# Low parts of the gate projections' weights: by a subtraction on VectorE, or by transfers that add the raw weights to the negated high part

## The chip, the cores and the metric

The kernel runs on one core of a Trainium2 chip. Such a core has TensorE (PE) for matrix products, VectorE (DVE), ScalarE (ACT) and GpSimd (POOL) for elementwise work, SyncE (SP), which here only issues transfers, and 16 DMA engines. Each engine works through its own list of instructions in order; they wait for each other on semaphores. SyncE and GpSimd each have a queue of transfers of their own. The metric is the device time of one execution in microseconds (us), the median of several runs.

## The reference, cut to what matters

Two layers of a hybrid decoder trunk on 528 prompt tokens and 64 sample tokens (592 columns in all), in float32. One input projection of the normalized x yields queries, keys, values, the gates of two branches and two merging gates g_a and g_b:

```python
def mixer_layer(x, ...):
    xn = rmsnorm(x, ln_g)
    proj = xn @ w_in
    q, k, v, z_a, x_b, z_b, g_a, g_b = jnp.split(proj, SPLIT_IDX, axis=-1)
    ...
    o_a = group_norm(ret, gn_g).astype(x.dtype) * jax.nn.silu(z_a)
    xc, conv_new = causal_conv(x_b, conv_buf, cw, cb)
    h, h_last = rglru(xc, h0, w_r, b_r, w_i, b_i, lam)
    o_b = h.astype(x.dtype) * jax.nn.silu(z_b)
    merged = jax.nn.sigmoid(g_a) * (o_a @ w_a) + jax.nn.sigmoid(g_b) * (o_b @ w_b)
    return x + merged @ w_o, S_new, conv_new, h_last
```

The change concerns the weights of g_a and g_b: 2 x 1024 columns of w_in, 1024 deep, per layer.

## The kernel before

**Numbers in two parts.** Products of float32 are made from pairs: every operand is split in a high part, rounded to the type that TensorE multiplies (fp32r), and a low part, the rest. A product is then three matmuls: high by high, low by high, high by low (`three`, lines 1654 to 1659).

**The stream of weights.** All weights of a layer come as 124 units of 128 x 1024 numbers (512 KB) in the order in which they are used. There is a ring of four slots (RING = 4). SyncE loads unit u into slot u % 4 of `w_raw` as soon as TensorE has ended unit u - 4 (lines 541 to 552). ScalarE copies it to `w_hi` (`split_hi`, line 464), VectorE subtracts `w_hi` from `w_raw` (`split_lo`, line 472) and counts up the semaphore unit_lo, for which TensorE waits ahead of the unit (`wait_unit`). `w_lo` and `w_raw` are the same memory: the subtraction is done in place. Both splits of unit i + 3 stand, in each engine's list, behind the engine's own work on unit i.

**The phases of a layer** are R (four heads of retention, 16 units each), L (the convolution and the gated recurrence, 24 units in two passes), GA and GB (the projections g_a and g_b, 8 units each, numbered 88 to 103 within the layer), B (the product with w_b, 12 units) and O (w_o, 8 units). In GA and GB each unit makes two halves of 296 columns (288 in the last layer). ScalarE takes each half out of PSUM with a tanh into `sg` (`tanh_g`, line 934), which frees its bank; there are four banks, two units' worth, so unit 90 needs those of unit 88. VectorE multiplies `sg` of GA into `acc` (line 1552). In GB the same goes on, but first ScalarE makes the twelve high parts of `ob` (line 990) and VectorE the twelve low ones (line 1557).

**The end of phase L** reaches into GA. The last group's recurrence is three scans on VectorE (`scan`, lines 1493 to 1508); they need ScalarE's exponentials and roots (lines 974 to 984), which follow ScalarE's splits of units 90 and 91. The third scan stands behind VectorE's split of unit 92.

**GpSimd's list** at that place, which is also the order of its transfers: the transfers that mix tiles for the gates of the recurrence (`mixes`, line 662), a wait for the last scan (ob_ready), then four transfers: the old x to `xT` (2368 KB), the next layer's parameters, the convolution outputs and the recurrence outputs to DRAM; then a wait until the latter two have been stored (lru_out), then, in layer 0, a wait for the new x (lines 686 to 699).

```python
act.wait_ge(unit_in[n % RING], arrived(l * UNITS_LAYER + it * p.units + p.unit0 + n))
act.activation(w_hi[:, n % RING, :], w_raw[:, n % RING, :], ACT.Copy).then_inc(unit_hi, 1)
...
dve.wait_ge(unit_hi, l * UNITS_LAYER + it * p.units + (p.unit0 + n + 1))
dve.tensor_tensor(w_lo[:, n % RING, :], w_raw[:, n % RING, :], w_hi[:, n % RING, :].bitcast(f32),
                  SUB).then_inc(unit_lo, 1)
```

Of the kernel before, what the change touches and what calls it, by code (L numbers as in the profile page):

```python
# [46 lines left out]
RING = 4  # L47
# [174 lines left out]
def trunk(nc, x_in, w_units, gate_w, packs, final_gain, consts, decay, state_ret,  # L222
          y_out, ret_p, ret_s, conv_out, h_out):
    f32, f32r = mybir.dt.float32, mybir.dt.float32r
    ALU, ACT = mybir.AluOpType, mybir.ActivationFunctionType
    MUL, ADD, SUB = ALU.mult, ALU.add, ALU.subtract
# [3 lines left out]
    with ctx:  # L230
# [3 lines left out]
        def keep(name, shape, dt=f32):  # L234
            at = (top[0] + 31) // 32 * 32
            top[0] = at + int(np.prod(shape[1:])) * 4
            return nc.alloc_sbuf_tensor_at(name, shape, dt, offset=at)
# [5 lines left out]
        w_hi = keep("w_hi", [P, RING, 1024], f32r)  # L243
        top[0] = (top[0] + 31) // 32 * 32
        w_raw = alias("w_raw", top[0], [P, RING, 1024])
        w_lo = keep("w_lo", [P, RING, 1024], f32r)
# [113 lines left out]
        def sem(name):  # L360
            return ctx.enter_context(nc.semaphore(name))

        unit_in = [sem(f"unit_in{i}") for i in range(RING)]
        unit_hi, unit_lo, unit_done = sem("unit_hi"), sem("unit_lo"), sem("unit_done")
# [1 line left out]
        bank_free = [sem(f"bank_free{i}") for i in range(RING)]  # L366
        const_in, trig_in, ones_ready, x_ready, x_stored, x_again = (sem(n) for n in (
            "const_in", "trig_in", "ones_ready", "x_ready", "x_stored", "x_again"))
        gain_in = sem("gain_in")
        xgh_ready, xg_ready = sem("xgh_ready"), sem("xg_ready")  # L370
        x_init = [sem(f"x_init{i}") for i in range(len(LOADS))]
        first_in, first_hi_ready, first_lo_ready, eps_ready = (sem(n) for n in (
# [45 lines left out]
        def apart(eng):  # L418

            eng.sem_inc(passed, 1)  # L420
# [33 lines left out]
        def v_bank(j):  # L454
            return psum_of("R", ("v", j)) if j < 4 else v_last

        def split_hi(act, ph, l, it, i):

            p = PH[ph]
            n = i + AHEAD  # L460
            if l * UNITS_LAYER + it * p.units + p.unit0 + n >= UNITS:
                return
            act.wait_ge(unit_in[n % RING], arrived(l * UNITS_LAYER + it * p.units + p.unit0 + n))
            act.activation(w_hi[:, n % RING, :], w_raw[:, n % RING, :], ACT.Copy).then_inc(unit_hi, 1)  # L464

        def split_lo(dve, ph, l, it, i):
            p = PH[ph]
            n = i + AHEAD
            if l * UNITS_LAYER + it * p.units + p.unit0 + n >= UNITS:
                return  # L470
            dve.wait_ge(unit_hi, l * UNITS_LAYER + it * p.units + (p.unit0 + n + 1))
            dve.tensor_tensor(w_lo[:, n % RING, :], w_raw[:, n % RING, :], w_hi[:, n % RING, :].bitcast(f32),  # L472
                              SUB).then_inc(unit_lo, 1)
# [96 lines left out]
        def _(pool):  # L570
# [13 lines left out]
            for l in range(0, DEPTH):  # L584
# [80 lines left out]
                def mixes(g):  # L665
                    gg = l * GROUPS + g
                    pool.wait_ge(gw_free, l * 6 + g + 2)
                    for tiles_done, parts in ((2, ((0, 0, 96, 128), (0, 1, 0, 96), (1, 1, 64, 128))), (3, ((1, 2, 0, 64),))):
                        for which, ready in enumerate((xch_ready, xcl_ready)):
                            pool.wait_ge(ready, gg * 3 + tiles_done)  # L670
                            apart(pool)
                            for to, tile, r0, r1 in parts:
                                mix(g, to, tile, r0, r1, which)
# [9 lines left out]
                load_gates(3)  # L683
                mixes(2)
                mixes(3)
                pool.wait_ge(ob_ready, l * LT + LT)
                apart(pool)
                pool.dma_start(xT[:, :, :].rearrange("p k t -> p (k t)"), x_in if l == 0 else x_scr[l - 1])\
# [5 lines left out]
                               h_new[:, :, :].rearrange("p a b -> p (a b)")).then_inc(lru_out, 16)  # L694
                pool.wait_ge(lru_out, l * 32 + 32)
                pool.sem_inc(lru_left, 1)
                if l + 1 < DEPTH:
                    pool.wait_ge(x_ready, l * KT + KT)
                    pool.dma_start(x_scr[l], acc[:, :, :].rearrange("p k t -> p (k t)")).then_inc(x_stored, 16)
# [1414 lines left out]
```

## Time and profile before

| | |
|---|---|
| median of 3 runs | 1926.42 us (1926.24 to 1926.42) |
| the profiled execution | 1926.77 us |
| its span, from the first to the last instruction | 1924.9 us |
| TensorE busy | 1904.5 us, 99% of the span |
| VectorE busy | 1187.7 us, 62% |
| ScalarE busy | 760.9 us, 40% |
| GpSimd busy | 267.5 us, 14% |
| GpSimd's transfers | 95.22 MB, 14.9% of the engines' time |
| SyncE's transfers | 149.71 MB, 24.9% |

The times of busy engines overlap, so they don't add up to the span. The engine that is busy throughout sets it; of the others one has to ask whether it ever makes that one wait. A timeline row reads: start, duration, engine, line of the program, operation, result and operands with their shapes, and in brackets how long the engine stood idle before it and what ended that. A line of waits reads: engine, what it was about to do, for whom it waited; the total, how many times, and the longest. Transfers issued by GpSimd have a row of their own for the issue; the time from there to the landing of the last byte is listed with the transfers.

### The profile page before, as it was taken

What the parts mean: (1) busy time and instruction counts of PE and PEld (TensorE: products, weight loads), DVE (VectorE), ACT (ScalarE), POOL (GpSimd) and SP (SyncE); (2) the same over time, 40 slices, a digit from 0 to 9 for tenths busy, and PEclk for the clock granted to TensorE, in tenths of its full rate; (3) what the DMA queues carried; (4) which work ended last, traced back from release to release, by engine and by line L of the source; (5) the groups of instructions that cost most, each with busy time, mean ns of one, the idle gap of its engine ahead of it and who ended that gap; (6) DMA issues with size and microseconds to landing.
All of it is one profiled execution on the core that took longest, in us unless ns stands there. A gap on an engine that the chain in (4) does not pass through costs nothing.

```text
span 1924.9 us, 32032 instructions
## 1 busy us (share of the span) xinstructions
PE 1904.5 (99%) x13112; PEld 1782.1 (93%) x13112; DVE 1187.7 (62%) x2008; ACT 760.9 (40%) x1181; POOL 267.5 (14%) x375
## 2 busy tenths in 40 slices
PE   8999999999999999999999999999999999999998
PEld 7889898898899999999998988988988999999997
DVE  8775665665766887424487656657557678763345
ACT  5432322323327776422344223233123377754223
POOL 2221120120231200000022201202102422000000
PEclk9999999999999999999999999999999999999999
DMA  6435534453443433322254435534444533342222
GB/s 216 133 117 164 169 136 127 161 174 111 146 149 93 114 99 113 113 77 77 88 172 156 139 127 171 171 114 146 164 127 135 163 102 110 92 138 77 87 79 82
DMA packets 105857, 246.99 MB, mean 128 GB/s; under 512 B 10830, under 2 KB 51262, under 8 KB 105326
## 3 DMA queue, kind: packets, MB, share of 16 engines
q1 hardware_dynamic: 78590, 149.71, 24.9%
q0 software_dynamic: 26976, 95.22, 14.9%
q8 instruction: 104, 1.70, 0.4%
q14 instruction: 43, 0.35, 0.1%
q10 hardware_dynamic: 144, 0.00, 0.0%
HBM read 186.07 MB, written 49.12 MB: 122 GB/s over the span
## 4 chain that ended last, share of the span: by engine, by line
PE 85%; DVE 5%; ACT 4%; DVEq 2%; DMA 1%; ACTq 1%; issue 1%; SPq 0%
PE bank L1657 21%; PE bank L1659 20%; PE bank L1658 20%; PE bank L1727 4%; PE bank L1729 4%; PE bank L1728 4%; PE last L1745 1%; PE last L1727 1%; PE last L1729 1%; PE last L1728 1%; PE sums L1852 1%; PE sums L1854 1%; PE sums L1856 1%; PE bank L1908 1%; PE sums L1763 1%
## 5 line engine op out<-in xcount | busy, mean ns | idle before, releaser
L1657 PE MATMUL bank<-xn_hi,w_hi 128*128 128x296 f32 (+1 forms) x2432 | 726.7, 299 | 0.2
L1659 PE MATMUL bank<-xn_lo,w_hi 128*128 128x296 f32 (+1 forms) x2432 | 722.3, 297 | 0.0
L1658 PE MATMUL bank<-xn_hi,w_lo 128*128 128x296 f32 (+1 forms) x2432 | 721.5, 297 | 0.0
L1657 PEld LDWEIGHTS bank<-xn_hi,w_hi 128*128 128x128 f32 x2432 | 457.3, 188 | 6.6 <-issue 4.3
L1658 PEld LDWEIGHTS bank<-xn_hi,w_lo 128*128 128x128 f32 x2432 | 457.7, 188 | 1.1
L1659 PEld LDWEIGHTS bank<-xn_lo,w_hi 128*128 128x128 f32 x2432 | 456.8, 188 | 0.0
L472 DVE TENSOR_TENSOR w_lo<-w_raw,w_hi 128x1024 fp32r<-128x1024 f32 x245 | 300.3, 1228 | 186.2 <-ACT w_hi L464 179.3
L464 ACT ACTIVATE w_hi<-w_raw 128x1024 fp32r<-128x1024 f32 x245 | 257.8, 1055 | 353.8 <-DMA w_raw<-in_w_units 349.3
L1657 PE MATMUL bank<-oa_hi,w_hi 128*128 128x296 f32 (+1 forms) x512 | 153.7, 300 | 0.0
L1658 PE MATMUL bank<-oa_hi,w_lo 128*128 128x296 f32 (+1 forms) x512 | 151.9, 297 | 0.0
L1659 PE MATMUL bank<-oa_lo,w_hi 128*128 128x296 f32 (+1 forms) x512 | 151.7, 296 | 0.0
L1657 PE MATMUL bank<-ob_hi,w_hi 128*128 128x296 f32 (+1 forms) x384 | 113.9, 297 | 0.0
L1658 PE MATMUL bank<-ob_hi,w_lo 128*128 128x296 f32 (+1 forms) x384 | 113.9, 297 | 0.0
L1659 PE MATMUL bank<-ob_lo,w_hi 128*128 128x296 f32 (+1 forms) x384 | 113.8, 296 | 0.0
L1727 PE MATMUL bank<-w_hi,xn_hi 128*128 128x512 f32 x256 | 100.8, 394 | 0.7 <-DVE rot_k L1191 0.7
L1729 PE MATMUL bank<-w_lo,xn_hi 128*128 128x512 f32 x256 | 100.8, 394 | 0.0
L1728 PE MATMUL bank<-w_hi,xn_lo 128*128 128x512 f32 x256 | 100.7, 393 | 0.0
L1657 PEld LDWEIGHTS bank<-oa_hi,w_hi 128*128 128x128 f32 x512 | 96.3, 188 | 3.9 <-issue 3.9
L1658 PEld LDWEIGHTS bank<-oa_hi,w_lo 128*128 128x128 f32 x512 | 96.3, 188 | 0.0
L1659 PEld LDWEIGHTS bank<-oa_lo,w_hi 128*128 128x128 f32 x512 | 96.3, 188 | 0.0
L606 POOL DMA_DIRECT2D out_ret_s<-S x64 | 46.0, 721 | 326.5 <-DVEq L1142 181.4
L781 ACT ACTIVATE zz<-bank 128x296 f32<-128x296 f32 (+1 forms) x64 | 26.6, 415 | 133.3 <-PE bank L1659 132.7
(293 smaller groups left out, 3069.0 us busy)
## 6 DMA issues: line engine op xcount, KB each, us to landing
w_raw<-in_w_units SPq DMA_DIRECT2D x215, 512.0 KB, 3.6
S<-in_state_ret POOLq DMA_DIRECT2D x64, 512.0 KB, 4.7
out_ret_s<-S POOLq DMA_DIRECT2D x64, 512.0 KB, 6.3
w_raw<-in_w_units SPq DMA_DIRECT2D x66, 256.0 KB, 3.3
vst<-v_scr SPq DMA_DIRECT2D x8, 512.0 KB, 4.0
out_ret_p<-Sp POOLq DMA_DIRECT2D x8, 512.0 KB, 5.7
v_scr<-vtok_hi SPq DMA_DIRECT2D x16, 160.0 KB
dec<-in_decay POOLq DMA_DIRECT2D x9, 264.0 KB, 5.0
```

What stands on the lines that cost most here:

```text
L464: act.activation(w_hi[:, n % RING, :], w_raw[:, n % RING, :], ACT.Copy).then_inc(unit_hi, 1)
L472: dve.tensor_tensor(w_lo[:, n % RING, :], w_raw[:, n % RING, :], w_hi[:, n % RING, :].bitcast(f32), SUB).then_inc(unit_lo, 1)
L606: pool.dma_start(dst, S[:, s, :, :]).then_inc(s_out[s], 16)
L781: act.activation(zz[:, i - 8, a:b], psum_of("R", name)[:, 0:b - a], ACT.Tanh, scale=0.5)\
L1657: pe.matmul(ps, w_hi[:, slot, cols], x_hi, start=first, stop=False)
L1658: pe.matmul(ps, w_lo[:, slot, cols], x_hi, start=False, stop=False)
L1659: return pe.matmul(ps, w_hi[:, slot, cols], x_lo, start=False, stop=last)
L1727: pe.matmul(ps, left_hi, right_hi, start=first, stop=False)
L1728: pe.matmul(ps, left_lo, right_hi, start=False, stop=False)
L1729: return pe.matmul(ps, left_hi, right_lo, start=False, stop=last)
L1745: ins = pe.matmul(o_last[at:at + QUAD, :], qz[:, c, b * QUAD:b * QUAD + QUAD], S[:, s, c, :], start=(n < 4 and c == 0), stop=(n >= 4 and c ...
L1763: return pe.matmul(to[:, :], kst[rows, b // 4, c * P:c * P + P], vst[rows, b // 4, :], start=True, stop=True)
```

## The change

In units 88 to 103 of each layer the low part is made in another way. ScalarE, behind the high part, drains and writes the negated high part over the raw weights (`w_lo`, the same memory). GpSimd then issues a transfer that reads the raw weights of the unit from DRAM a second time and adds them to what is there, so that raw minus high is left. VectorE no longer subtracts in these units; at the same place in its list it waits for the transfer and passes it on to TensorE by counting up unit_lo. The adds of the first five units stand in GpSimd's list ahead of its wait for the last scan, the other eleven behind the wait for the stores.

```diff
--- before.py
+++ after.py
@@ -366,7 +366,7 @@
         bank_free = [sem(f"bank_free{i}") for i in range(RING)]
         const_in, trig_in, ones_ready, x_ready, x_stored, x_again = (sem(n) for n in (
             "const_in", "trig_in", "ones_ready", "x_ready", "x_stored", "x_again"))
-        gain_in = sem("gain_in")
+        gain_in, minus_hi, lo_in = sem("gain_in"), sem("minus_hi"), [sem(f"lo_in{i}") for i in range(RING)]
         xgh_ready, xg_ready = sem("xgh_ready"), sem("xg_ready")
         x_init = [sem(f"x_init{i}") for i in range(len(LOADS))]
         first_in, first_hi_ready, first_lo_ready, eps_ready = (sem(n) for n in (
@@ -454,6 +454,11 @@
         def v_bank(j):
             return psum_of("R", ("v", j)) if j < 4 else v_last
 
+        GATED = range(PH["GA"].unit0, PH["GB"].after[1])
+
+        def gated(l, at):
+            return l * len(GATED) + at - GATED.start
+
         def split_hi(act, ph, l, it, i):
 
             p = PH[ph]
@@ -462,11 +467,19 @@
                 return
             act.wait_ge(unit_in[n % RING], arrived(l * UNITS_LAYER + it * p.units + p.unit0 + n))
             act.activation(w_hi[:, n % RING, :], w_raw[:, n % RING, :], ACT.Copy).then_inc(unit_hi, 1)
+            if it * p.units + p.unit0 + n in GATED:
+                act.drain()
+                act.activation(w_lo[:, n % RING, :], w_hi[:, n % RING, :].bitcast(f32), ACT.Copy, scale=-1.0)\
+                   .then_inc(minus_hi, 1)
 
         def split_lo(dve, ph, l, it, i):
             p = PH[ph]
             n = i + AHEAD
             if l * UNITS_LAYER + it * p.units + p.unit0 + n >= UNITS:
+                return
+            if it * p.units + p.unit0 + n in GATED:
+                dve.wait_ge(lo_in[n % RING], 16 * (gated(l, it * p.units + p.unit0 + n) // RING + 1))
+                dve.sem_inc(unit_lo, 1)
                 return
             dve.wait_ge(unit_hi, l * UNITS_LAYER + it * p.units + (p.unit0 + n + 1))
             dve.tensor_tensor(w_lo[:, n % RING, :], w_raw[:, n % RING, :], w_hi[:, n % RING, :].bitcast(f32),
@@ -683,6 +696,15 @@
                 load_gates(3)
                 mixes(2)
                 mixes(3)
+
+                def add_raw(at):
+                    pool.wait_ge(minus_hi, gated(l, at) + 1)
+                    apart(pool)
+                    pool.dma_start(w_lo[:, at % RING, :], w_units[l * UNITS_LAYER + at], accum_op=ADD)\
+                        .then_inc(lo_in[at % RING], 16)
+
+                for at in GATED[0:5]:
+                    add_raw(at)
                 pool.wait_ge(ob_ready, l * LT + LT)
                 apart(pool)
                 pool.dma_start(xT[:, :, :].rearrange("p k t -> p (k t)"), x_in if l == 0 else x_scr[l - 1])\
@@ -694,6 +716,8 @@
                                h_new[:, :, :].rearrange("p a b -> p (a b)")).then_inc(lru_out, 16)
                 pool.wait_ge(lru_out, l * 32 + 32)
                 pool.sem_inc(lru_left, 1)
+                for at in GATED[5:]:
+                    add_raw(at)
                 if l + 1 < DEPTH:
                     pool.wait_ge(x_ready, l * KT + KT)
                     pool.dma_start(x_scr[l], acc[:, :, :].rearrange("p k t -> p (k t)")).then_inc(x_stored, 16)
```

In GpSimd's list, from the last mixing transfers of layer 0 to the end of the layer, stood before:

```order
L662 DMA mix_hi<-xc_hi 64x592 [waits xch_ready]
L662 DMA mix_lo<-xc_lo 64x592 [waits xcl_ready]
L688 DMA xT<-in_x 128x4736 [waits ob_ready]
L690 DMA lp<-in_packs 128x504
L691 DMA out_conv<-conv_new 128x324
L693 DMA out_h<-h_new 128x108
L699 DMA x_scr<-acc 128x4736 [waits lru_out,x_ready]
```

and stands now:

```order
L675 DMA mix_hi<-xc_hi 64x592 [waits xch_ready]
L675 DMA mix_lo<-xc_lo 64x592 [waits xcl_ready]
L703 DMA w_lo<-in_w_units 128x1024 [waits minus_hi] x5
L710 DMA xT<-in_x 128x4736 [waits ob_ready]
L712 DMA lp<-in_packs 128x504
L713 DMA out_conv<-conv_new 128x324
L715 DMA out_h<-h_new 128x108
L703 DMA w_lo<-in_w_units 128x1024 [waits lru_out,minus_hi]
L703 DMA w_lo<-in_w_units 128x1024 [waits minus_hi] x10
L723 DMA x_scr<-acc 128x4736 [waits x_ready]
```

The wait for the stores (lru_out) has moved from the transfer of the new x to the add of unit 93.

In VectorE's list, from the end of the second scan of the last group (layer 0) through the third to the first products with `sg`, stood before:

```order
L1508 SCALAR_TENSOR_TENSOR ob<-rr,zl 128x592
L472 TENSOR_TENSOR w_lo<-w_raw,w_hi 128x1024 [waits unit_hi]
L1493 TENSOR_TENSOR ii<-ii,rr 128x592 [waits sqrt_ready]
...
L1508 SCALAR_TENSOR_TENSOR ob<-rr,ob 128x592
L1552 SCALAR_TENSOR_TENSOR acc<-sg,acc 128x296 [waits ga_ready] x4
L472 TENSOR_TENSOR w_lo<-w_raw,w_hi 128x1024 [waits unit_hi]
```

and stands now:

```order
L1532 SCALAR_TENSOR_TENSOR ob<-rr,zl 128x592
L1517 TENSOR_TENSOR ii<-ii,rr 128x592 [waits lo_in0,sqrt_ready]
...
L1532 SCALAR_TENSOR_TENSOR ob<-rr,ob 128x592
L1576 SCALAR_TENSOR_TENSOR acc<-sg,acc 128x296 [waits ga_ready] x4
L1576 SCALAR_TENSOR_TENSOR acc<-sg,acc 128x296 [waits lo_in1,ga_ready]
```

The subtraction for unit 92 has gone from between the scans, and its place is taken by a wait for the add of unit 92 (lo_in0) ahead of the third scan; that for unit 93 (lo_in1) stands among the products.

In ScalarE's list, where the high parts of units 90 and 91 are made in layer 0, stood before:

```order
L917 ACTIVATE ii<-bank,lp 128x592 [waits psum_full]
L464 ACTIVATE w_hi<-w_raw 128x1024 [waits unit_in2]
L464 ACTIVATE w_hi<-w_raw 128x1024 [waits unit_in3]
L917 ACTIVATE rr<-sums,lp 64x592 [waits psum_full]
```

and stands now:

```order
L941 ACTIVATE ii<-bank,lp 128x592 [waits psum_full]
L469 ACTIVATE w_hi<-w_raw 128x1024 [waits unit_in2]
L472 ACTIVATE w_lo<-w_hi 128x1024
L469 ACTIVATE w_hi<-w_raw 128x1024 [waits unit_in3]
L472 ACTIVATE w_lo<-w_hi 128x1024
L941 ACTIVATE rr<-sums,lp 64x592 [waits psum_full]
```

Each high part is followed by its negation, ahead of the gates of the recurrence.

## Rows read from the trace of the kernel before

**Rows 1.** The page, busy time (share of the span) and instructions of each engine.

```profile
PE 1904.5 (99%) x13112; PEld 1782.1 (93%) x13112; DVE 1187.7 (62%) x2008; ACT 760.9 (40%) x1181; POOL 267.5 (14%) x375
```

**Rows 2.** The waits of TensorE: us in total, times, longest us.

```profile
PE bank L1657 <- DVE xg_lo L1063: 1.8, 2, 1.1
...
PE last L1727 <- DVE w_lo L472: 0.7, 1, 0.7
```

**Rows 3.** The page, costliest groups: busy us, mean ns | idle before, releaser.

```profile
L472 DVE TENSOR_TENSOR w_lo<-w_raw,w_hi 128x1024 fp32r<-128x1024 f32 x245 | 300.3, 1228 | 186.2 <-ACT w_hi L464 179.3
```

**Rows 4.** Timeline of TensorE: first matmuls of units 88, 90, 92, 93, 99; layer 1: 93, 99.

```profile
735.94 0.30 PE L1657 MATMUL bank<-xn_hi,w_hi 128*128 128x296 f32 x1
...
748.98 0.30 PE L1657 MATMUL bank<-xn_hi,w_hi 128*128 128x296 f32 x1
...
762.02 0.30 PE L1657 MATMUL bank<-xn_hi,w_hi 128*128 128x296 f32 x1
...
768.54 0.30 PE L1657 MATMUL bank<-xn_hi,w_hi 128*128 128x296 f32 x1
...
807.66 0.30 PE L1657 MATMUL bank<-xn_hi,w_hi 128*128 128x296 f32 x1
...
1715.89 0.29 PE L1657 MATMUL bank<-xn_hi,w_hi 128*128 128x288 f32 x1
...
1754.13 0.29 PE L1657 MATMUL bank<-xn_hi,w_hi 128*128 128x288 f32 x1
```

**Rows 5.** Timeline of ScalarE around GA and GB, layer 0, then layer 1.

```profile
736.71 2.01 ACT L464 ACTIVATE w_hi<-w_raw 128x1024 fp32r<-128x1024 f32 x2
...
748.00 0.40 ACT L934 ACTIVATE sg<-bank 128x296 f32<-128x296 f32 x1
...
754.78 1.06 ACT L464 ACTIVATE w_hi<-w_raw 128x1024 fp32r<-128x1024 f32 x1
...
798.09 1.06 ACT L464 ACTIVATE w_hi<-w_raw 128x1024 fp32r<-128x1024 f32 x1
...
1702.92 1.06 ACT L464 ACTIVATE w_hi<-w_raw 128x1024 fp32r<-128x1024 f32 x1
...
1744.82 1.06 ACT L464 ACTIVATE w_hi<-w_raw 128x1024 fp32r<-128x1024 f32 x1
```

**Rows 6.** The page, DMA issues: KB of each, median us from issue to landing.

```profile
S<-in_state_ret POOLq DMA_DIRECT2D x64, 512.0 KB, 4.7
```

**Rows 7.** Stretch with xT: each engine's busy us, PEclk, DMA share, GB/s.

```profile
763.00:770.00 7.00, 7.00 (x53) 7.00 (x53) 5.50 (x11) 2.38 (x4) 2.22 (x4) 1.00 0.93 321
```

**Rows 8.** Timeline of GpSimd, layer 0, then layer 1.

```profile
729.16 0.52 POOL L662 DMA_DIRECT2D mix_lo<-xc_lo  x1 [0.28 <-issue]
763.83 0.58 POOL L688 DMA_DIRECT2D xT<-in_x  x1 [34.15 <-DVE ob L1508]
...
765.50 0.55 POOL L693 DMA_DIRECT2D out_h<-h_new  x1
...
1711.90 0.58 POOL L688 DMA_DIRECT2D xT<-x_scr  x1 [34.14 <-DVE ob L1508]
...
1713.57 0.55 POOL L693 DMA_DIRECT2D out_h<-h_new  x1
```

**Rows 9.** Timeline of VectorE: first instruction of the third scan, layer 0.

```profile
759.64 0.78 DVE L1493 TENSOR_TENSOR ii<-ii,rr 128x592 f32<-128x592 f32 x1
```

**Rows 10.** DMA issues in 760 to 790 us, then in 1708 to 1735 us.

```profile
out_h<-h_new POOLq DMA_DIRECT2D x1, 54.0 KB, 11.4
...
out_h<-h_new POOLq DMA_DIRECT2D x1, 54.0 KB, 9.8
```

**Rows 11.** Last stretches: busy us (PE first), then PEclk, DMA share, GB/s.

```profile
1916.00:1917.00 1.00, 0.39 (x2) 0.00 (x0) 0.04 (x1) 0.51 (x2) 0.00 (x0) 1.00 0.12 40
...
1919.00:1920.00 1.00, 0.00 (x0) 0.00 (x0) 1.00 (x2) 0.00 (x0) 0.00 (x0) 1.00 0.00 0
1920.00:1921.00 1.00, 0.00 (x0) 0.00 (x0) 1.00 (x2) 0.00 (x0) 0.00 (x0) 0.86 0.31 115
1921.00:1921.50 0.50, 0.00 (x0) 0.00 (x0) 0.50 (x2) 0.00 (x0) 0.00 (x0) 0.50 1.06 362
```

## The prediction

> **What bounds the kernel now.** I read the table of busy times first, then the waits of TensorE, then the timeline of each engine around the gate units of layer 0 (735 to 808 us) and of layer 1 (1684 to 1754 us). TensorE is busy for 99% of the span [rows 1]. Its waits are tiny: the longest sum in the list is 1.8 us, and the one wait for a low part in a stage after the first units is 0.7 us in total [rows 2]. So nothing that VectorE gives up can shorten the run by more than a microsecond or so; the question is only whether the new way of making the low parts is ever late. A unit that comes late stops TensorE, and nearly all of that delay goes to the end, since TensorE has no idle time elsewhere in which to make it up.
>
> I call the sixteen gate units of a layer 88 to 103, as the code numbers them. **What is removed:** 32 subtractions on VectorE, 1.23 us each [rows 3], 39 us of VectorE's time. VectorE is busy for 62% [rows 1], and TensorE hardly waits for it, so I price this at zero.
>
> **The deadlines.** From TensorE's timeline: unit 88 starts at 735.94, 90 at 748.98, 92 at 762.02, 93 at 768.54 and 99 at 807.66; in layer 1, 93 starts at 1715.89 and 99 at 1754.13 [rows 4]. A unit lasts 6.52 us in layer 0 and 6.37 in layer 1 (the second follows from 1715.89 and 1754.13, six units apart).
>
> **What is added on ScalarE:** behind each high part a wait for its own result and a second pass of the same size, 1.06 us [rows 5], with its drain 1.1 us. In the middle of the sixteen this is nothing, because ScalarE idles there. At the head it is not: the high parts of 90 and 91 are made back to back from 736.71, and everything behind them follows without a gap up to the high part of 92 at 754.78 [rows 5]. So from there ScalarE runs 2.2 us later. The first sigmoid-gate evacuation (line 934) moves from 748.00 to 750.2 and frees its bank at 750.6, where TensorE wants it at 748.98 for unit 90 [rows 4, 5]: a first delay of 1.6 us. The high part of 92 begins at 757.0 instead of 754.78, its negation ends at 759.2.
>
> **What is added on the transfer queue:** 32 accumulating transfers of 512 KB, issued by GpSimd. The trace has no such transfer. The nearest rows: plain loads of 512 KB that GpSimd issues take 4.7 us from issue to landing [rows 6]. That is the lower bound, since the new ones move the same bytes. An accumulating transfer has to read its destination too. Between 763 and 770 us the engines moved 321 GB/s at a share of 0.93, so 345 GB/s when fully busy [rows 7]; one more reading of 512 KB is then 1.5 us, which gives 6.2 us. The upper bound is a transfer of twice the whole plain time, 9.4 us. I take **L = 6.2 us**: start-up and completion are paid once, only the movement doubles.
>
> The Trainium skill bears on this in two places. "DMA: Bandwidth & Descriptors" (Anatomy of one DMA — SWDGE (gpsimd) path) fits a GpSimd-issued transfer as about 2.0 us plus bytes over 436 GB/s, which would be 3.2 us here; this trace says 4.7, and the trace decides. "Collectives: The Full Stack" (The bandwidth ceiling: the fold count and why AG ≠ RS ≠ AR) says that an add in the transfer engines halves the rate because it needs two source reads, not because adding costs time; by it and the fit together L would be an estimated 4.4 us (3.2 and another 1.2 for the second reading), and the sum below, with its four L, some 7 us smaller. No row of this trace shows an add, so the rule is untested here.
>
> **What is moved: the place of the transfers in GpSimd's order.** This is the term that decides. GpSimd handles its list strictly in order. The adds of 88 to 92 stand ahead of its wait for the last scan; the add of 93 stands behind it, and behind the wait until the convolution and recurrence outputs have been stored (lru_out). Before, no one cared how late that was.
>
> Unit 88: GpSimd is busy with the last mixing transfer until 729.7 [rows 8]; 729.7 + 6.2 = 735.9, against 735.94. A few tenths at most, which the 1.6 us of ScalarE's shift cover. Units 89 to 91 have 6.5 us more each. VectorE now stands waiting for the adds of 88 to 91 until about 748, but the work behind it waits for ScalarE until about then anyway.
>
> Unit 92: negated at 759.2, add issued 759.3, landed 765.5, VectorE goes on at 765.6. TensorE, already 1.6 us late, wanted it at 763.6, so it is now 3.7 us late. More important is what is queued behind VectorE's wait: the third scan. It began at 759.64 [rows 9] and GpSimd issued the first of its four transfers at 763.83 [rows 8], 4.2 us later. Now: 765.6 + 4.2 = 769.8.
>
> Unit 93: the four transfers (xT, lp, conv, h) are issued one after the other, the last at 765.50, 1.67 us after the first [rows 8], and that last one landed 11.4 us after its issue [rows 10], together 13.1 us, since it stands behind 2.4 MB of xT. 769.8 + 13.1 = 782.9: the add of 93 is issued. + 6.2 = 789.1, + 0.2 for VectorE's passing it on = 789.3. It was wanted at 768.54: **TensorE is 20.8 us late**, the 3.7 us and 1.6 us included. It stands idle from about 772 to 789. In terms of L this is 8.4 + 2 L, as two adds lie one behind the other on the path.
>
> Layer 1 in the same way: high part of 92 at 1702.92 + 2.2 = 1705.1 [rows 5], negated 1707.3, landed 1713.6, VectorE 1713.7, GpSimd 1717.9. There the four transfers took from 1711.90 to 1713.57 + 9.8 [rows 8, 10], 11.5 us: 1729.4. Add landed 1735.6, TensorE 1735.8 against 1715.89 [rows 4]: **19.9 us late**, or 7.5 + 2 L.
>
> Units 94 and 95 were negated long before and their adds follow that of 93 directly; even at 3 us between landings they are in time. From 96 on the chain is: TensorE ends unit i, ScalarE evacuates, makes high part and negation of i+3 (done 2.8 us after the end), the add takes 6.2: 9.2 us with the passing on, of the 13.0 us (two units) that there are. Hidden, with 3.8 us to spare; what uses that up is L above 10 us.
>
> Unit 99 is the exception, because ScalarE first makes the twelve high parts of ob. Its own high part began at 798.09 [rows 5], now 799.2; negated 801.4, landed 807.7, passed on 807.9, wanted 807.66: 0.2 us. In layer 1, 1744.82 [rows 5] leads to 1754.6 against 1754.13 [rows 4]: 0.5 us. Together 0.7.
>
> **The clock.** After the last matmuls of the kernel (two of them in 1916 to 1917) the granted clock stays at 1.00 until 1920 and then falls to 0.50, as the mean of 0.86 in 1920 to 1921 tells [rows 11]: 2.4 GHz, then 1.2 GHz, some 4 us after the last work. In a hole of 17 us the same must happen, and TensorE starts unit 93 at half speed. How fast it comes back no row shows. Bounds: nothing, and one whole unit at half speed, 6.5 us. If the clock rises about as quickly as it fell, it costs half of 4 us: I take 2 us a layer, 4 in all.
>
> **The sum.** 20.8 + 19.9 + 0.7 + 4.0 = 45.4 us. The profiled execution took 1926.77 us (span 1924.9), which is within 0.4 of the median 1926.42. 1926.8 + 45.4 = **1972 us**.
>
> **Rivals.**
> (a) The adds are much slower than any row suggests, L = 14 us. Then the head costs 36.4 + 35.5, and the steady part no longer hides: each three units lose 14 + 3 - 13 = 4 us, unit 99 about 8, some 16 us a layer. 1926.8 + 72 + 32 + 4 = 2035 us. For: nothing in the trace adds in a transfer. Against: the bytes. It decides from L = 10 on.
> (b) The add of 93 isn't held up: GpSimd's wait for the stores is over in time and only ScalarE's 1.6 us a layer stays. 1930 us. Against: even on the times of before, the stores landed at 765.50 + 11.4 = 776.9, 8.4 us after unit 93 began, so this needs a wrong reading of GpSimd's order.
> (c) The other side, a little faster: all adds hidden, and VectorE's freed 39 us take away TensorE's small waits. The place is the head of each layer's recurrence, where VectorE is crowded; but the gated subtractions come after most of it. At most 1 us: 1926 us, no change. It decides only if (b) holds as well and ScalarE's shift is absorbed.
> (d) The change doesn't do what it says, for example VectorE still subtracts or the adds aren't there. The instruction lists show 16 adds a layer and no subtraction in their place, so this has no chance worth a number.
>
> **How the numbers follow.** Forecast 0.85, (a) 0.11, (b) 0.02, (c) 0.02, of which half would read as faster at all. The forecast's own range: L = 4.7 and no cost of the clock give 17.8 + 16.9 = 34.7, so 1961; L = 9.4 gives 27.2 + 26.3, unit 99 a further 7, and the clock up to 13: 73.5, so 2000. I widen it a little to both sides, for stores that land sooner or later than before and for a part of (a): 1958 to 2006. A measurement of this kernel can tell about 0.2% from no change, 3.9 us. Faster 0.01, the same 0.02, slower 0.97.
>
> **What will show it.** Right: in the waits, TensorE stands once per layer for some 17 us ahead of its first instruction on unit 93, near 772 to 789, and again near 1742 to 1758 in layer 1, whose clock times are some 23 us later by then; in the waits of VectorE two long ones, for the adds of 92 and 93; GpSimd's first add behind out_h about 13 us after xT was issued; the adds' time from issue to landing near 6 us; the granted clock at 0.50 in the hole and for a few us after it; unit 96 to 98 with no wait. Wrong: TensorE's hole missing; adds landing in under 4.7 us or over 10 us; many waits of some 4 us spread over the gate units (then (a)); a hole that costs no clock.

## The result, and the profile after

| | before | after |
|---|---|---|
| median | 1926.42 us (1926.24 to 1927.38, 4 runs) | 1972.88 us (1970.94 to 1977.13, 4 runs) |
| the profiled execution | 1926.77 us | 1972.85 us |
| TensorE busy | 1904.5 us, 99% | 1911.3 us, 97% |
| VectorE busy | 1187.7 us | 1151.5 us |
| ScalarE busy | 760.9 us | 793.9 us |

The kernel became slower: the ratio after to before is 1.0243, 95% interval 1.0225 to 1.0261. The forecast was 1972 us, 1958 to 2006. The 36 us that VectorE gave up bought nothing, and TensorE stood some 40 us longer. The costliest groups of the page after (busy us, mean ns | idle before, releaser) and its transfers (KB, median us from issue to landing):

```profile
L1681 PE MATMUL bank<-xn_hi,w_hi 128*128 128x296 f32 (+1 forms) x2432 | 729.8, 300 | 39.4 <-DVEq L482 38.6
...
L485 DVE TENSOR_TENSOR w_lo<-w_raw,w_hi 128x1024 fp32r<-128x1024 f32 x213 | 261.2, 1229 | 156.5 <-ACT w_hi L469 100.6
...
w_lo<-in_w_units POOLq DMA_DIRECT2D x32, 512.0 KB, 5.7
```

The subtraction on VectorE [rows 3] is down from 245 to 213 times. L482 is the line in which VectorE counts up unit_lo after an add has landed, and it ends 38.6 of the 39.4 us in which TensorE stood before a unit's first matmul. The waits of TensorE and VectorE after (total us, times, longest), against [rows 2]:

```profile
DVE acc L1576 <- DMA w_lo<-in_w_units: 87.8, 12, 17.4
...
PE bank L1681 <- DVEq L482: 38.6, 8, 15.8
```

Where the eight are, the timeline of TensorE says (start, duration, ..., idle before and releaser). These are the first matmuls of units 88, 90, 92, 93 and 99 of layer 0, then 88, 90, 92, 93 and 99 of layer 1, against [rows 4]:

```profile
737.18 0.41 PE L1681 MATMUL bank<-xn_hi,w_hi 128*128 128x296 f32 x1 [1.19 <-DVEq L482]
...
750.69 0.37 PE L1681 MATMUL bank<-xn_hi,w_hi 128*128 128x296 f32 x1 [0.20 <-ACT sg L958]
...
765.21 0.41 PE L1681 MATMUL bank<-xn_hi,w_hi 128*128 128x296 f32 x1 [1.24 <-DVEq L482]
...
787.03 0.61 PE L1681 MATMUL bank<-xn_hi,w_hi 128*128 128x296 f32 x1 [15.04 <-DVEq L482]
...
829.58 0.41 PE L1681 MATMUL bank<-xn_hi,w_hi 128*128 128x296 f32 x1 [0.49 <-DVEq L482]
...
1707.44 0.40 PE L1681 MATMUL bank<-xn_hi,w_hi 128*128 128x288 f32 x1 [1.53 <-DVEq L482]
...
1720.99 0.38 PE L1681 MATMUL bank<-xn_hi,w_hi 128*128 128x288 f32 x1 [0.54 <-ACT sg L958]
...
1735.46 0.40 PE L1681 MATMUL bank<-xn_hi,w_hi 128*128 128x288 f32 x1 [1.48 <-DVEq L482]
...
1757.90 0.61 PE L1681 MATMUL bank<-xn_hi,w_hi 128*128 128x288 f32 x1 [15.80 <-DVEq L482]
...
1800.15 0.40 PE L1681 MATMUL bank<-xn_hi,w_hi 128*128 128x288 f32 x1 [1.79 <-DVEq L482]
```

Two rows carry 31 of the 39 us: one hole per layer, both before unit 93. What leads to the hole in layer 0 stands in the chain of work that released unit 93 (start, duration, what; "DMA" runs from the end of the waiting to the landing):

```profile
758.09 1.07 ACT w_lo L472
759.20 0.53 issue
759.72 5.39 DMA w_lo<-in_w_units
...
765.30 0.78 DVE ii L1517
...
766.49 1.39 DVE rr L1526
...
768.19 0.69 DVE ob L1532
768.92 0.55 issue
769.47 0.56 POOL xT L710
...
771.10 9.51 DMA out_h<-h_new
...
780.75 0.54 issue
781.31 5.63 DMA w_lo<-in_w_units
786.96 0.03 DVEq L482
...
787.03 0.61 PE bank L1681
```

Read from the top: ScalarE ends the negation of unit 92; its add lands 5.4 us after the issue; only then does VectorE begin the third scan (765.30, against 759.64 in [rows 9]); GpSimd issues its four transfers; the last one lands 9.5 us after its issue; only then is the add of unit 93 issued; 5.6 us later TensorE may go on. Of the computation in these rows only the first is new. The rest of the chain is two adds, and between them a wait that nobody had to care about before.

### The profile page after: what moved, and what is told of

It is laid out like the page before. It is cut to its first block, busy times and chain, and to the rows that moved or that the text cites. A ratio compares the mean times of both kernels' runs of the same rounds, so it can differ in the third digit from the quotient of the medians.

```text
span 1971.0 us, 32160 instructions
## 1 busy us (share of the span) xinstructions
PE 1911.3 (97%) x13112; PEld 1786.7 (91%) x13112; DVE 1151.5 (58%) x1976; ACT 793.9 (40%) x1213; POOL 295.4 (15%) x407
## 4 chain that ended last, share of the span: by engine, by line
PE 78%; ACT 6%; DVE 6%; DMA 4%; ACTq 2%; issue 2%; DVEq 2%; SPq 0%; POOL 0%; POOLq 0%
PE bank L1681 19%; PE bank L1683 18%; PE bank L1682 18%; PE bank L1751 4%; PE bank L1753 4%; PE bank L1752 4%; DMA w_lo<-in_w_units 2%; PE last L1769 1%; PE last L1751 1%; PE last L1753 1%; PE last L1752 1%; DMA out_h<-h_new 1%; ACT w_hi L469 1%; PE sums L1876 1%; PE sums L1878 1%
## 5 line engine op out<-in xcount | busy, mean ns | idle before, releaser
L1681 PE MATMUL bank<-xn_hi,w_hi 128*128 128x296 f32 (+1 forms) x2432 | 729.8, 300 | 39.4 <-DVEq L482 38.6
L485 DVE TENSOR_TENSOR w_lo<-w_raw,w_hi 128x1024 fp32r<-128x1024 f32 x213 | 261.2, 1229 | 156.5 <-ACT w_hi L469 100.6
```

Source lines behind the costliest of these rows:

```text
L1681: pe.matmul(ps, w_hi[:, slot, cols], x_hi, start=first, stop=False)
```

## The experiments

The runs came in three groups. Those of a group were on one chip and share runs of the kernel before on it: 1926.22 us for the four on all adds first, the wait behind, the scan first and the passes alone; 1926.05 us for xT behind, the transfers without addition, TensorE kept busy (its first run) and the part without six units; 1926.19 us for the last three (the two repeats and the six units alone). Ratios are to that. Which line numbers a kernel has depends on its edit: "DVEq L482" is VectorE's passing on, "sg" ScalarE's evacuation of a bank.

The theory (T): the place of the adds in GpSimd's list makes the holes, by way of the chain above; ScalarE's second pass, the time of one add and the clock are small terms. The rivals: (R1) it is the adding itself, which is slow in the DMA engines; (R2) it is ScalarE's second passes; (R3) it is the clock that the holes cost.

### All adds ahead of the wait for the last scan

```diff
-                for at in GATED[0:5]:
+                for at in GATED:
                     add_raw(at)
...
                 pool.sem_inc(lru_left, 1)
-                for at in GATED[5:]:
-                    add_raw(at)
```

> All sixteen adds of a layer stand ahead of GpSimd's wait for the last scan and of the four transfers. My theory: both holes of 15 us go and the clock stays at full speed; what is left are the short waits of the kernel as changed, ahead of 88 (1.2 and 1.5 us), 90 (0.2 and 0.5), 92 (1.2 and 1.5) and 99 (0.5 and 1.8), 8.4 us in all: 1935 us. Rival, that the adds are too slow for two units' time (13 us): waits of several us at each of 94 to 98 as well, over 1950 us.

Measured: 1939.35 us (1937.32 to 1943.0), ratio 1.007 (1.0056 to 1.0084). The same 32 adds and the same passes of ScalarE, in another place, cost 13.1 us instead of 46.5. The waits of TensorE in this kernel:

```profile
PE bank L1679 <- DVEq L482: 6.4, 6, 1.4
PE bank L1679 <- DVE w_lo L485: 2.2, 2, 1.1
...
PE bank L1679 <- ACT sg L956: 1.1, 2, 0.8
```

There is no hole any more. What is left is 6.4 us for late adds (88, 92 and 99), 1.1 us for banks, and a new one, 2.2 us for a subtraction: the raw weights of unit 105 come late, since xT's 2.4 MB now move beside them. The row of ScalarE's timeline in layer 0:

```profile
842.66 1.06 ACT L469 ACTIVATE w_hi<-w_raw 128x1024 fp32r<-128x1024 f32 x1 [4.68 <-DMA w_raw<-in_w_units]
```

Unit 105 counts here since TensorE waits for units 104 and 105 together at the head of phase B. This rules out R1 and R2 as the main cause: both are whole in this kernel. The median came out some 4 us above what T expected. The three waits sum to 9.7 us; the profiled execution, at 1937.32 us the fastest of the four, was 11.1 us slower than before. What the slower ones spent beyond that no trace shows.

### The wait for the stores moved behind the adds

```diff
-                pool.wait_ge(lru_out, l * 32 + 32)
-                pool.sem_inc(lru_left, 1)
                 for at in GATED[5:]:
                     add_raw(at)
+                pool.wait_ge(lru_out, l * 32 + 32)
+                pool.sem_inc(lru_left, 1)
```

> The wait for the stores (lru_out) is moved behind the adds of units 93 to 103; the four transfers (xT, lp, conv, h) stay ahead of them. My theory: about half of the hole ahead of unit 93 goes, because the add no longer waits for a completion, but it stays behind 2.4 MB of xT in the same queue. xT was issued at 769.5 and took 9.0 us; the add then lands near 781 to 782 instead of 787, so 5 to 6 us less per layer: 1961 to 1963 us. Rival, that transfers of one queue don't hold each other up: the add lands 5.7 us after its issue at 771.7, so near 777.4, 9.6 us less per layer: 1953 us. Rival, that GpSimd's order is not the cause (the adds' own cost is): no change, 1973 us.

Measured: 1965.51 us (1964.55 to 1967.64), ratio 1.0205 (1.0191 to 1.0219). GpSimd's timeline around 771 us, and the issues between 769 and 773 us (KB, us to landing):

```profile
771.28 1.85 POOL L703 DMA_DIRECT2D w_lo<-in_w_units  x2
```

```profile
xT<-in_x POOLq DMA_DIRECT2D x1, 2368.0 KB, 9.4
w_lo<-in_w_units POOLq DMA_DIRECT2D x2, 512.0 KB, 13.1
```

The adds are now issued 10 us sooner (771.28 against 781.31), but the first two land 13.1 us later, not 5.7. They stand behind xT in the same queue, and at 1965.5 us the kernel is a little slower than the 1961 to 1963 that were expected. Unit 93 still waits 11.85 us (12.93 in layer 1). So of the 46.5 us the wait instruction itself accounts for 7; what the instruction waits for, the 2.4 MB ahead, does its harm in either place. To read the hole as "it waits for a semaphore" would have been wrong: moving the wait away doesn't move the bytes away.

### xT behind the adds

```diff
                 apart(pool)
-                pool.dma_start(xT[:, :, :].rearrange("p k t -> p (k t)"), x_in if l == 0 else x_scr[l - 1])\
-                    .then_inc(x_again, 16)
...
                 for at in GATED[5:]:
                     add_raw(at)
+                pool.dma_start(xT[:, :, :].rearrange("p k t -> p (k t)"), x_in if l == 0 else x_scr[l - 1])\
+                    .then_inc(x_again, 16)
```

> Only the transfer of 2.4 MB to xT is moved, behind the adds of 93 to 103; the stores and the wait for them stay ahead of these. My theory: the stores took 9.5 us because they stand behind xT in the queue; alone they land some 4 us after their issue, and one issue of 0.55 us goes as well, so the add of 93 goes out 6 us sooner: 12 us less for both layers, 1961 us, less about 2 us that xT costs where it now stands (at the end of the adds, beside a load of raw weights, as in the kernel with the adds first). Rival, that the stores are slow by themselves: 1973 us.

Measured: 1959.15 us (1957.67 to 1961.84), ratio 1.0174 (1.0158 to 1.0189). GpSimd and TensorE at unit 93:

```profile
770.46 0.57 POOL L713 DMA_DIRECT2D out_h<-h_new  x1
774.50 2.67 POOL L703 DMA_DIRECT2D w_lo<-in_w_units  x3 [3.48 <-DMA out_h<-h_new]
```

```profile
779.94 0.61 PE L1681 MATMUL bank<-xn_hi,w_hi 128*128 128x296 f32 x1 [8.08 <-DVEq L482]
```

Without xT ahead of it the add of 93 is issued 4.0 us after the last store's issue, not 10.2 us (771.10 to 781.31), and the hole shrinks from 15.04 to 8.08 us. The loss is 33.1 us, so 13.4 of the 46.5 are xT's bytes ahead of the stores, less what xT costs where it now stands.

### The third scan ahead of VectorE's wait for unit 92

```diff
-                split_lo(dve, "GA", l, 0, 1)
                 scan(1, 1, 2)
+                split_lo(dve, "GA", l, 0, 1)
```

> Only VectorE's order is changed: the third scan stands ahead of its passing on of unit 92, as it can be done by then. GpSimd's order is that of the changed kernel. My theory: the link from the add of 92 to the third scan carries 4.7 us of each layer (VectorE stood 4.73 and 4.72 us there), so the four transfers and the add of 93 all come that much sooner: 9 us less, 1963 us. Rival, that the scan isn't in the chain: 1973 us.

Measured: 1965.45 us (1963.91 to 1967.85), ratio 1.0202 (1.0187 to 1.0218). GpSimd's timeline:

```profile
764.31 0.55 POOL L710 DMA_DIRECT2D xT<-in_x  x1 [4.25 <-DVE ob L1532]
...
765.94 0.56 POOL L715 DMA_DIRECT2D out_h<-h_new  x1
778.72 2.67 POOL L703 DMA_DIRECT2D w_lo<-in_w_units  x3 [12.21 <-DMA out_h<-h_new]
```

Counted from the issue of the add of 92 (759.21 here, 759.72 in the changed kernel), xT goes out 4.7 us sooner, as expected. The add of 93 doesn't go out 4.7 us sooner: from the issue of out_h to that of the add it is now 12.8 us, before it was 10.2. So the add of 93 moves by only 2.1 us (2.7 in layer 1). By the medians VectorE's wait ahead of the scan is worth some 7 us in all, of which TensorE's waits for adds show 4.9 (33.7 us against 38.6); about half of the sooner start is given back in the queue. What slows the stores there no run separates; the raw weights of SyncE's queue move at that time.

### ScalarE's second passes alone

```diff
+            if it * p.units + p.unit0 + n in GATED:
+                act.activation(w_hi[:, n % RING, :], w_raw[:, n % RING, :], ACT.Copy)
+                act.drain()
             act.activation(w_hi[:, n % RING, :], w_raw[:, n % RING, :], ACT.Copy).then_inc(unit_hi, 1)
```

This is an edit of the kernel before. The high part of these units is made twice, there are no adds, and VectorE subtracts as before.

> ScalarE's extra passes alone: each of the 32 units' high parts is made twice, with a drain between; no adds, VectorE subtracts as before. My theory: 2.2 us later on ScalarE at the head of GA frees the bank of unit 88 late for unit 90 by 1.7 us (layer 0) and 1.9 us (layer 1): 1930 us. Rival, that the ScalarE passes are hidden everywhere: 1926.4 us; rival, that they cost their own 34 us: 1960 us.

Measured: 1931.21 us (1929.88 to 1934.79, 7 runs), ratio 1.0027 (1.0016 to 1.0038). The wait is where it should be, before unit 90 of either layer:

```profile
PE bank L1672 <- ACT sg L949: 3.9, 2, 2.3
```

R2 is worth 4 to 5 us, a tenth. In the changed kernel nearly all of it is covered: unit 88 is late there by itself, so that TensorE wants the bank later.

### The addition taken out of the transfers

```diff
-                    pool.dma_start(w_lo[:, at % RING, :], w_units[l * UNITS_LAYER + at], accum_op=ADD)\
+                    pool.dma_start(w_lo[:, at % RING, :], w_units[l * UNITS_LAYER + at])\
```

The transfers write the raw weights over the negated high part, so what is left out is the addition, and with it the right low parts; order and bytes written are the same.

> The 32 transfers are plain loads of the same 512 KB in place of adds; this leaves out the addition, so the low parts are the raw weights. My theory: the cost of adding is the difference of 5.7 to 4.8 us in landing, and it stands twice in each layer's chain: some 4 us less, 1969 us. Rival, that the addition is what makes the kernel slower: back below 1940 us.

Measured: 1964.63 us (1961.91 to 1966.65), ratio 1.02 (1.0186 to 1.0213). The transfers of this kernel's page, and its waits of TensorE:

```profile
w_lo<-in_w_units POOLq DMA_DIRECT2D x32, 512.0 KB, 3.9
```

```profile
PE bank L1681 <- DVEq L482: 28.4, 3, 14.6
...
PE bank L1681 <- ACT sg L958: 3.6, 2, 1.9
```

Plain transfers land after 3.9 us, adding ones after 5.7: adding costs 1.8 us each. I had expected half of that, as I took the plain one to be 4.8 like the loads of S. Two adds per layer lie on the path to unit 93, so 4 x 1.8 = 7.2 us, and 7.9 were measured (46.5 less this kernel's 38.6). R1 is real and small: with free additions the kernel would still be 38.6 us slower than before. And the 3.6 us of ScalarE's banks come back as soon as unit 88 is in time.

### TensorE kept busy ahead of unit 93

```diff
                         for i in range(4):
+                            if (ph, it, i) == ("GA", 1, 1):
+                                pe.wait_ge(gate_free, 24 * (l + 1))
+                                for _ in range(105):
+                                    pe.matmul(sums[0][:, 0:HALF], xn_hi[:, 0, 0:P], xn_hi[:, 0, 0:HALF],
+                                              start=True, stop=True)
                             project(ph, l, it, ("proj", i), i)
```

The products are used by nobody. They fill the hole, so what is left out is the clock's fall alone.

> As the kernel as changed, but TensorE runs 105 products of 128 x 296 into a free bank ahead of its wait for unit 93, some 14 us of work that nobody uses, where it stood idle for 15.0 and 15.8 us. My theory of the clock: it stays at full speed, and unit 93, which took 5.9 us and 4.2 us at 1.2 GHz in the two layers, gives back half of that: 3.0 + 2.1 = 5 us less, 1968 us. Rival, that the half-speed stretch is hidden by something else that is late (units 94 and 95's adds): no change, 1973 us. Rival, that the extra products run over the wait: longer.

Measured: 1969.93 us (1968.55 to 1973.14), ratio 1.023 (1.0216 to 1.0244). Its distance to the 1972.88 of the changed kernel is no larger than the latter's own spread, so both were run again together:

> The kernel as changed once more, so that the next run is compared with it on the same chip: 1972 us, between 1970 and 1977 as before.

> The same kernel as e5_kept_busy (products that nobody uses in TensorE's hole ahead of unit 93), beside the changed kernel on one chip. Theory of the clock: 5 us less than that one, from half of the 5.9 and 4.2 us that unit 93 takes at 1.2 GHz. Rival, that part of it is hidden: 3 us less or under, as the first comparison over two chips had it.

Measured: the changed kernel 1973.71 us (1973.11 to 1974.11), ratio 1.0247 (1.0233 to 1.0261); with the products 1967.85 us (1967.7 to 1969.86), ratio 1.0219 (1.0205 to 1.0233). The difference is 5.9 us. It is the clock's share and a little more: unit 93 of layer 0 started 0.9 us sooner in the profile of the second. In the first pair part of the gain was lost: in that run's profile with the products, unit 88 of layer 1 came 3.0 us late, and after it the granted clock was 0.61 in 1706 to 1708 and 0.54 in 1708 to 1710. The second profile shows no such stretch. In stretches (us, PE busy first, then the other engines, then PEclk, DMA share, GB/s), the first profile of the changed kernel, then the second one with the products:

```profile
774.00:776.00 2.00, 0.00 (x0) 0.00 (x0) 0.00 (x0) 0.85 (x1) 0.00 (x0) 0.96 0.94 403
776.00:777.00 1.00, 0.00 (x0) 0.00 (x0) 0.00 (x0) 0.00 (x0) 0.00 (x0) 0.50 1.17 495
787.00:788.00 1.00, 0.97 (x4) 0.97 (x5) 0.84 (x2) 0.00 (x0) 0.00 (x0) 0.50 1.11 221
792.00:793.00 1.00, 1.00 (x6) 1.00 (x5) 0.84 (x2) 0.00 (x0) 0.00 (x0) 0.54 0.00 0
793.00:795.00 2.00, 2.00 (x17) 2.00 (x16) 0.00 (x0) 0.42 (x1) 0.00 (x0) 1.00 0.00 0
```

```profile
776.00:777.00 1.00, 1.00 (x10) 1.00 (x9) 0.00 (x0) 0.00 (x0) 0.00 (x0) 1.00 0.95 407
786.00:788.00 2.00, 1.45 (x10) 1.45 (x11) 0.84 (x2) 0.00 (x0) 0.00 (x0) 1.00 0.96 184
```

In the changed kernel TensorE's last matmul ends at 772.0; the mean of 0.96 in 774 to 776 says that the granted clock went from 1.00 to 0.50 (2.4 to 1.2 GHz) at about 775.8. It is 0.50 when unit 93 starts, and back at 1.00 from 792.9 on, after 5.9 us of work at half speed (4.4 us in layer 1). In the timeline the matmuls start 0.25 us apart at 0.50 and 0.14 us apart at 1.00 (0.24 and 0.13 in layer 1), so some 45% of that time is lost, a little less than the half that was expected: 2.6 + 2.0 = 4.6 us. R3 is a tenth of the loss by the trace and an eighth by the two runs.

### Adds only where they are hidden

Here only a part of the sixteen units keeps the new way; the others are subtracted as before. (Not shown: the counts of the semaphores follow the new list, and VectorE drains ahead of the first passing on behind a subtraction.) First units 93 to 98 and 100 to 103, with 93 to 98 ahead of the four transfers and the rest behind the stores:

```diff
-        GATED = range(PH["GA"].unit0, PH["GB"].after[1])
+        GATED = [u for u in range(PH["GA"].unit0 + 5, PH["GB"].after[1]) if u != PH["GB"].unit0 + 3]
...
-                for at in GATED[0:5]:
+                for at in GATED[0:6]:
                     add_raw(at)
```

> The new way only where the timeline shows it hidden: units 93 to 98 and 100 to 103 of each layer, with the six adds of 93 to 98 ahead of the four transfers and the wait for the stores, four behind them. Units 88 to 92 and 99 are subtracted on VectorE as before. My theory: no wait of TensorE is added, and the 20 subtractions that VectorE no longer does (25 us) gain nothing: 1926 to 1927 us, the same as before. Rival, that VectorE's freed time is worth something: under 1924 us. Rival, that a second read of the weights or the transfers' presence costs something everywhere: over 1930 us.

Measured: 1929.09 us (1927.91 to 1929.58, 11 runs), ratio 1.0014 (1.0005 to 1.0023). I had expected no wait at all. TensorE waits 1.8 us for two adds, those of unit 100, whose raw weights came late in either layer. The load of unit 100 in layer 0 and what ScalarE waited for it:

```profile
w_raw<-in_w_units SPq DMA_DIRECT2D x1, 512.0 KB, 9.8
...
803.61 1.06 ACT L472 ACTIVATE w_hi<-w_raw 128x1024 fp32r<-128x1024 f32 x1 [2.79 <-DMA w_raw<-in_w_units]
```

In the kernel before the load of that unit took 3.4 us. Here xT, which the six adds ahead of it have moved to 791.24, goes through the DMA engines at that time; in layer 1 the load took 12.0 us, and ScalarE waited 5.11 us. The 1.2 us that the time is above the two waits no trace places. Then 93 to 98 alone:

```diff
-        GATED = range(PH["GA"].unit0, PH["GB"].after[1])
+        GATED = list(range(PH["GA"].unit0 + 5, PH["GB"].unit0 + 3))
```

> The new way for units 93 to 98 alone (12 of the 32), all ahead of the four transfers. In e8 the waits of TensorE that remained, 0.8 and 1.0 us, stood ahead of unit 100, whose add came behind the transfers. Theory: without it nothing is left, 1926 us, the same as before. Rival, that the transfers' place or the double reading costs by itself what e8 showed beyond its two waits (about 1.2 us): 1927 to 1928 us.

Measured: 1926.32 us (1925.83 to 1927.46, 11 runs), ratio 1.0001 (0.9992 to 1.001). TensorE waits for no add in it, and 0.2 us for one subtraction; the raw weights of unit 100 are as late as in the last run, but a subtraction is done in time behind them. VectorE has 12 subtractions less (1174.5 us busy against 1187.7), and the time is that of before. Both halves of the trade are seen here: adds that are not late cost nothing that can be measured, and the 13 us that VectorE is freed of bring nothing. I found no version that beats the kernel before, and its waits leave none to be expected of this kind.

## Why the prediction was right, step by step

**What bounds the kernel.** Right. VectorE's freed time at zero is borne out by the last run, for 12 of the 32 subtractions.

**The time of one add, L.** Forecast 6.2 us, measured 5.4 and 5.65 on the path in layer 0, 5.7 as the median. Both parts of my working were off, and the errors went against each other: a plain load in this place takes 3.9 us, not 4.7, and the adding costs 1.8 us, not 1.5. By the fit in the Trainium skill, "DMA: Bandwidth & Descriptors" (Anatomy of one DMA — SWDGE (gpsimd) path), the plain one would take an estimated 3.2 us; the trace of the run without addition says 3.9. The Trainium skill, "Collectives: The Full Stack" (The bandwidth ceiling: the fold count and why AG ≠ RS ≠ AR), puts the add's cost in the second reading of its sources. The 1.8 us between the adding and the plain transfers are more than the 1.2 us that I estimated from the two pages: the direction agrees and the size is the measurement's.

**Unit 88.** Forecast a few tenths late, measured 1.19 and 1.53 us. This is the step that failed most in proportion. The working used L for an add alone, but the adds of 88 and 89 are issued back to back, behind the mixing transfers and beside a load of raw weights. The median of the two from issue to landing was 8.4 us, that of 88 by itself 7.5:

```profile
w_lo<-in_w_units POOLq DMA_DIRECT2D x2, 512.0 KB, 8.4
w_raw<-in_w_units SPq DMA_DIRECT2D x1, 512.0 KB, 6.9
```

It cost nothing in the sum, since the 1.6 us of ScalarE's shift were to come right after: units 88 and 90 together are 1.4 and 2.1 us late.

**ScalarE's shift.** Right: alone it gives 1.6 and 2.3 us (the run with the passes only), and the negation of 92 ends at 759.16, forecast 759.2.

**Unit 92 and the third scan.** Forecast 3.7 us late with the scan's first instruction at 765.6; measured 3.2 (765.21 against 762.02) and 765.30. The 4.2 us from there to GpSimd's first transfer held exactly (769.47). What I left out is 0.53 us from the negation's end to the start of the issue on GpSimd; 0.54 us like it stand between the landing of the stores and the issue of the add of 93.

**The four transfers.** Forecast 13.1 and 11.5 us from the first issue to that of the add of 93, taken from the landings of before. Measured 11.8 us in layer 0 (769.47 to 781.31) and 12.8 us in layer 1 (1739.67 to 1752.49). The sum of the two is right, but either one is 1.3 us off, one each way, and that they cancel is luck. As the run with the scan first showed, this time isn't a constant that one may carry along: from the issue of xT to that of the add it was 14.4 us when xT started some 5 us sooner.

**Unit 93.** Forecast 20.8 us late, measured 787.03 against 768.54 = 18.5 us. For layer 1 the forecast was 19.9; the waits from unit 88 to unit 93 sum to 1.53 + 0.54 + 1.48 + 15.80 = 19.4.

**Units 94 to 98.** Right: none of them waits. **Unit 99.** Forecast 0.2 and 0.5 us, measured 0.49 and 1.79. In layer 1 the negation ended where forecast, but the adds took 7.2 us.

**The clock.** Forecast 2 us a layer by "it rises about as quickly as it fell"; measured 2.6 and 2.0. In this kernel it fell 3.9 and 3.1 us after the last matmul and came back after 5.9 and 4.4 us of work, so the rise took longer than the fall; the forecast had them equal.

**The sum.** TensorE's waits for adds and banks are 38.6 + 0.7 = 39.3 us, the clock 4.6: 43.9. The difference between the profiled executions is 46.1. The remaining 2.2 us I can only partly place: the first matmul behind each of the ten waits takes 0.37 to 0.61 us in place of 0.30, some 1.4 us together. The forecast was 45.4: up to unit 93 the two layers came out 2.3 and 0.5 us shorter than forecast, unit 99 1.6 us and the clock 0.6 us longer. The mechanism and its place were right, and the closeness of the last figure is partly luck: the errors of the terms went both ways.

**The rivals.** L of 14 us: not seen, the adds' median is 5.7 us. The add of 93 not held up: the hole is there. No change: this is what a kernel with six hidden adds does, not this one.

## What to carry to other kernels

When work moves from an engine to a queue, first ask what stands ahead of it in that queue's order, the waits as well as the bytes: the same 32 transfers cost 46 us with eleven of each layer's sixteen behind a wait for stores and 2.4 MB, and 13 us ahead of them; the six per layer that fit cost nothing. And those 2.4 MB are a burden wherever they go: moved behind six or sixteen adds they made a load of raw weights late. Where an engine that works in order then waits for the late piece, look at what stands behind that wait; here the third scan did, and through it the next transfer's own release. And offload only from an engine for which the bounding engine really waits: with TensorE at 99% and 0.7 us of waits for low parts, the best that could come out was no change.

## What the runs showed of the hardware

- An accumulating transfer of 512 KB from DRAM into on-chip memory took 5.7 us from issue to landing, a plain one in the same place 3.9 us. GpSimd is busy with the issue for 0.85 us in place of 0.53. I had not expected the issue itself to be dearer.
- What stands ahead in the same queue counts: two adds behind 2368 KB in GpSimd's queue landed 13.1 us after their issue (the median of all adds was 5.7), and between the issue of the 54 KB store and that of the add which waited for it lay 10.2 to 12.8 us behind the 2368 KB, 4.0 us without them.
- Moving xT never made it free. Sooner, the stores slowed. Behind six adds, SyncE's load of the raw weights of unit 100 took 9.8 and 12.0 us in place of 3.4 and 3.9. Behind all the adds, the raw weights of unit 105 came 4.68 us after ScalarE wanted them.
- From the end of a ScalarE instruction to the start of the issue on GpSimd that it releases 0.53 us passed, and 0.54 us from the landing of the stores to the issue of the add.
- The granted clock fell 3.9 and 3.1 us after the last matmul in the first profile of the changed kernel, 1.9 and 4.2 us in the second. After the restart it stayed at its lower level for 5.9 and 4.4 us of work in the first, 3.8 and 5.1 in the second, 5.9 and 3.4 in the run with the wait behind the adds: it varies by more than 2 us from hole to hole.
